# The rows of experts 0 to 29 added under the last expert, the last two experts' tokens scattered over the output

## The reference

```python
x = x + merged @ w_o
x = x + hier_moe(rmsnorm(x, norm_ffn), ...)

def expert_block(args):
    xb, e = args
    return (jax.nn.silu(xb @ w_gate[e]) * (xb @ w_up[e])) @ w_down[e]
...
y = jnp.zeros((t + 1, d), jnp.float32).at[row_tok].add(out.astype(jnp.float32) * row_w[:, None])
```

## Time and profile before

| what | value |
|---|---|
| median of 3 runs | 2049.8 us (2048.38 to 2050.29) |
| the profiled execution | 2054.24 us |
| its span | 2052.4 us |
| PE busy over the span | 1842.6 us, 90% |
| DVE busy over the span | 1283.2 us, 63% |
| ACT busy over the span | 1006.8 us, 49% |
| POOL busy over the span | 639.4 us, 31% |

### The profile page before, as it was taken

How to read it: one execution, slowest core, us unless ns; L and a number is a source line. 1 busy time by engine, 2 the same in 40 slices (tenths; PEclk the granted TensorE clock), 3 DMA queues, 4 the chain that set the end, 5 groups by cost and what they waited for, 6 DMA issues and landing times. The chain is left out here.

```text
span 2052.4 us, 26125 instructions
## 1 busy us (share of the span) xinstructions
PE 1842.6 (90%) x9426; PEld 1420.9 (69%) x9426; DVE 1283.2 (63%) x1351; ACT 1006.8 (49%) x1579; POOL 639.4 (31%) x368
## 2 busy tenths in 40 slices
PE   4898999999999779899999898985999999999991
PEld 3777787787787645677888786444677777777771
DVE  2677866875884835433344354124888888888883
ACT  4244543533444431355675420122577787777761
POOL 5247646746754933100134431000010111111000
PEclk7999999999999978899999999986999999999996
DMA  3243452424335442231155444512899999999985
GB/s 110 66 128 91 118 141 80 129 85 131 109 107 147 134 160 57 70 126 37 44 183 168 145 154 150 229 72 84 302 355 374 372 375 366 378 370 372 375 301 199
DMA packets 228110, 379.50 MB, mean 185 GB/s; under 512 B 14576, under 2 KB 176624, under 8 KB 203312
## 3 DMA queue, kind: packets, MB, share of 16 engines
q1 hardware_dynamic: 220272, 363.45, 51.8%
q0 software_dynamic: 7168, 12.60, 1.8%
q10 hardware_dynamic: 576, 2.18, 0.3%
HBM read 333.94 MB, written 55.25 MB: 190 GB/s over the span
## 5 line engine op out<-in xcount | busy, mean ns | idle before, releaser
L2011 DVE TENSOR_TENSOR e_w_low<-e_raw,e_w_high 128x2048 fp32r<-128x2048 f32 x190 | 426.5, 2286 | 63.3 <-ACT e_w_high L2007 63.3
L523 POOL TENSOR_TENSOR w_w_low<-w_raw,w_w_high 128x1024 fp32r<-128x1024 f32 x92 | 250.4, 2722 | 456.0 <-ACT w_w_high L518 456.0
L2007 ACT ACTIVATE e_w_high<-e_raw 128x2048 fp32r<-128x2048 f32 x190 | 349.9, 1914 | 0.0
L185 PE MATMUL bank<-h_high,w_w_high 128*128 128x512 f32 (+1 forms) x912 | 320.7, 352 | 31.9 <-ACT ssd_conv_in L802 16.7
L185 PE MATMUL bank<-h_low,w_w_high 128*128 128x512 f32 (+1 forms) x912 | 312.2, 342 | 0.0
L185 PE MATMUL bank<-h_high,w_w_low 128*128 128x512 f32 (+1 forms) x912 | 311.7, 342 | 0.0
L185 PEld LDWEIGHTS bank<-h_high,w_w_high 128*128 128x128 f32 x912 | 178.4, 196 | 65.0 <-issue 29.9
L2023 PE MATMUL bank<-e_w_high,e_xT_high 128*96 128x512 f32 x512 | 206.8, 404 | 3.2 <-DVE e_xT_low L2101 1.6
L2023 PE MATMUL bank<-e_w_high,e_xT_low 128*96 128x512 f32 x512 | 203.2, 397 | 0.0
L2023 PE MATMUL bank<-e_w_low,e_xT_high 128*96 128x512 f32 x512 | 202.3, 395 | 0.0
L946 DVE SCALAR_TENSOR_TENSOR ssd_xc<-ssd_conv_in,ssd_conv_p,ssd_xc 128x774 f32<-128x774 f32 x144 | 194.7, 1352 | 10.8
(11 more groups left out here) (282 smaller groups left out, 3582.4 us busy)
## 6 DMA issues: line engine op xcount, KB each, us to landing
e_raw<-in_w_gate SPq DMA_DIRECT2D x64, 1024.0 KB, 7.6
e_raw<-in_w_up SPq DMA_DIRECT2D x64, 1024.0 KB, 7.6
e_raw<-in_w_down SPq DMA_DIRECT2D x64, 1024.0 KB, 6.9
w_raw<-in_w_in SPq DMA_DIRECT2D x68, 512.0 KB, 4.1
ssd_decays<-decay_sums SPq DMA_DIRECT2D x48, 512.0 KB, 6.6
projected<-ssd_side SPq DMA_DIRECT2D x33, 384.0 KB, 2.5
w_raw<-in_w_out_ssm SPq DMA_DIRECT2D x16, 512.0 KB, 4.1
y_ssd<-ssd_y SPq DMA_DIRECT2D x24, 256.0 KB, 2.4
```

The costliest lines, as they stand in the source:

```text
L185: last = pe.matmul(out, lhs[k][a], rhs[k][b], start=(k == 0 and m == 0), stop=(k == n - 1 and m == 2))
L523: pool.tensor_tensor(self.pair[u].low[:, :, :], self.raw[u][:, :, :], self.pair[u].high[:, :, :].bitcast(F32), ALU.subtract).then_inc(self ...
L2007: act.activation(pair[n].high[:, :], core.raw[c][:, :], ACT.Copy).then_inc(high_ok, 1)
L2011: dve.tensor_tensor(pair[n].low[:, :], core.raw[c][:, :], pair[n].high[:, :].bitcast(F32), ALU.subtract).then_inc(low_ok, 1)
```

## The change

It has four parts.

1. SP waits for the scatters of experts 0 to 29 only, and loads each tile of `y_rows` into the raw buffer that comes free next while the last expert runs (`ROW_AT`, `ROW_FREE`). To make room, the last expert's two w_down chunks go to raw buffers 0 and 1 (`load_chunk(..., into=c)`), and their rounding and lowering moves ahead in ACT's and DVE's program of the last expert.
2. The twelve additions are split: tiles 0 to 2 go to POOL, 3 to 5 to DVE (`add_rows`).
3. Experts 30 and 31 no longer write `y_rows`. For their tokens the whole result is made apart, in the expert's slots: POOL gathers the token's x1 row (from the new table `x1_rows`, stored in `mix_and_route`) and the row of the token's other choice, and DVE adds these two and y. Since a token may have both experts, y of expert 30 also goes to a table of its own, `y_late` (zeroed as `y_rows` is), from which expert 31 gathers. The indices for all that are made by eight small DVE operations (`late_rows`).
4. When all six tiles are stored, POOL scatters these rows over the stored output, expert 30's first, two DMAs each (one for each sequence; indices outside a sequence are skipped), and waits for each pair.

The core of the diff:

```diff
                 def zeros(c):
-                    rows = core.y_rows[:, c * ZW:(c + 1) * ZW].rearrange("(b p) z -> p b z", p=P)
+                    for table in (core.y_rows, core.y_late):
+                        rows = table[:, c * ZW:(c + 1) * ZW].rearrange("(b p) z -> p b z", p=P)
...
                         sp.dma_start(core.h2_rows[at:at + P, :], h2[t % 2][:, :]).then_inc(h2_out[t % 2], 16)
+                    sp.dma_start(core.x1_rows[t * P:(t + 1) * P, :], x[:, t, :]).then_inc(x1_out, 16)
...
+            if last:
+                for c in range(2):
+                    round_chunk(act, END[c], down(e, c, True), c, NEXP)
             if not first:
                 act_out(act, e - 1, 1 - u, i - (1 - u))
...
+            else:
+                for c in range(2):
+                    lower_chunk(dve, END[c], down(e, c, True), c)
             dve.wait_ge(hh_ok, e + 1)
...
+        def late_rows(dve):
...
+            then(dve.tensor_copy(late[0][:, :], core.slot_row[:, NEXP - 2:NEXP]))
+            then(dve.tensor_scalar(late[1][:, :], late[0][:, :], float(TOK), float(TOK), ALU.is_ge, ALU.mult))
+            then(dve.tensor_tensor(late[0][:, :], late[0][:, :], late[1][:, :], ALU.subtract))
+            dve.tensor_copy(late_token[:, :], late[0][:, :])
+            then(dve.scalar_tensor_tensor(late[1][:, :], late[1][:, :], -1.0, late[0][:, :], ALU.mult, ALU.add))
+            dve.tensor_scalar(late_other[:, :], late[1][:, :], float(TOK), None, ALU.add)
+            then(dve.tensor_scalar(late[2][:, :], late[0][:, :], float(SEQS[0]), NO_ROW, ALU.is_lt, ALU.mult))
+            dve.scalar_tensor_tensor(late_second[:, :], late[0][:, :], -float(SEQS[0]), late[2][:, :],
+                                     ALU.add, ALU.add).then_inc(late_ok, 1)
...
+        def late_store(pool, v):
+            for s, index in enumerate((late_token, late_second)):
+                pool.indirect_dma_start(
+                    out=core.out[s][0], out_offset=bass.IndirectOffsetOnAxis(ap=index[:, v:v + 1], axis=0),
+                    in_=x[v][:, :], in_offset=None,
+                    bounds_check=SEQS[s] - 1, oob_is_err=False).then_inc(late_stored, 16)
...
+        def add_rows(eng, t, done):
+            eng.wait_ge(pair_in[t], 16)
+            for n in range(2):
+                last = eng.tensor_tensor(core.x1[:, t, :], core.x1[:, t, :],
+                                         core.raw[ROW_AT[t]][:, n * D:(n + 1) * D], ALU.add)
...
+        POOL_TILES = tuple(range(NT // 2))
+        ROW_AT = (2, 3, 4, 5, 0, 1)
+        ROW_FREE = (gate_up(NEXP - 1, 2), gate_up(NEXP - 1, 3), down(NEXP - 2, 0), down(NEXP - 2, 1),
+                    down(NEXP - 1, 0, True), down(NEXP - 1, 1, True))
...
-                sp_expert(sp, NEXP - 1, ahead=0)
-                sp.wait_ge(low_ok, 6 * NEXP)
+                for c in range(2):
+                    sp.wait_ge(low_ok, gate_up(NEXP - 1, c) + 1)
+                    load_chunk(sp, core, NEXP - 1, 4 + c, into=c)
                 for u in range(2):
-                    sp.wait_ge(y_out[u], 16 * (NEXP // 2))
+                    sp.wait_ge(y_out[u], 16 * (NEXP // 2 - 1))
                 rows = core.y_rows.rearrange("(n t p) d -> t p n d", n=2, p=P)
                 for t in range(NT):
-                    sp.dma_start(core.raw[t][:, :].rearrange("p (n d) -> p n d", n=2), rows[t]).then_inc(pair_in[t], 16)
-                for t in range(NT):
-                    sp.wait_ge(sum_ok, t + 1)
+                    sp.wait_ge(low_ok, ROW_FREE[t] + 1)
+                    sp.dma_start(core.raw[ROW_AT[t]][:, :].rearrange("p (n d) -> p n d", n=2), rows[t])\
+                        .then_inc(pair_in[t], 16)
+                for t in (0, 1, 3, 2, 4, 5):
...
                     sp.dma_start(core.out_tile(t), core.x1[:, t, :]).then_inc(stored, 16)
-                sp.wait_ge(stored, 16 * NT)
...
-                for e in range(NEXP):
+                for e in range(NEXP - 2):
                     pool_expert(pool, e)
+
+                pool.wait_ge(late_ok, 1)
+                for u in range(2):
+                    pool.wait_ge(y_out[u], 16 * (NEXP // 2 - 1))
+                for v in range(2):
+                    pool.wait_ge(x_tr, NEXP - 1 + v)
+                    late_gather(pool, x[v], core.x1_rows, late_token[:, v:v + 1], TOK, base_in[v])
+                    late_gather(pool, other[v], core.y_rows, late_other[:, v:v + 1], 2 * TOK, base_in[v])
+                add_rows(pool, 0, pool_sum_ok)
...
+                add_rows(pool, 1, pool_sum_ok)
+                pool.wait_ge(y_out[0], 16 * (NEXP // 2))
+                pool.wait_ge(based, 2)
+                late_gather(pool, other[1], core.y_late, late_other[:, 1:2], 2 * TOK, late_in)
+                add_rows(pool, 2, pool_sum_ok)
+                pool.wait_ge(stored, 16 * NT)
+                for v in range(2):
+                    pool.wait_ge(final_ok, v + 1)
+                    late_store(pool, v)
+                    pool.wait_ge(late_stored, 32 * (v + 1))
...
+                late_rows(dve)
...
+                for v in range(2):
+                    dve.wait_ge(base_in[v], 32)
+                    dve.tensor_tensor(x[v][:, :], x[v][:, :], other[v][:, :], ALU.add).then_inc(based, 1)
+                dve.wait_ge(y_ok, NEXP - 1)
+                dve.drain()
+                dve.tensor_tensor(x[0][:, :], x[0][:, :], y[0][:, :], ALU.add).then_inc(final_ok, 1)
+                for t in range(len(POOL_TILES), NT):
+                    add_rows(dve, t, dve_sum_ok)
+                dve.wait_ge(late_in, 16)
+                dve.tensor_tensor(x[1][:, :], x[1][:, :], other[1][:, :], ALU.add)
+                dve.wait_ge(y_ok, NEXP)
+                dve.drain()
+                dve.tensor_tensor(x[1][:, :], x[1][:, :], y[1][:, :], ALU.add).then_inc(final_ok, 1)
```

More of the change, by code:

```diff
@@ L1103, in zeros @@
                 def zeros(c):
[L1104 to L1106 removed]
+                    for table in (core.y_rows, core.y_late):
+                        rows = table[:, c * ZW:(c + 1) * ZW].rearrange("(b p) z -> p b z", p=P)
+                        sp.dma_start(rows, core.zeros[:, :].unsqueeze(1).to_broadcast([P, 2 * NT, ZW]))\
+                            .then_inc(core.zero_out, 16)
                 for i in range(ATT_SIDES):
@@ L1952, in weight_chunks, with load_chunk @@
     return [sb(f"e_raw{c}", [P, CHUNK_COLS]) for c in range(CHUNKS)]
-def load_chunk(sp, core, e, c):
+def load_chunk(sp, core, e, c, into=None):
+    into = c if into is None else into
     name, k = (("w_gate", KD), ("w_up", KD), ("w_down", KE))[c // 2]
     rows = core.expert_rows(name, e, k)[:, (c % 2) * (k // 2):(c % 2 + 1) * (k // 2), :]
-    sp.dma_start(core.raw[c][:, :].rearrange("p (k n) -> p k n", k=k // 2), rows).then_inc(core.raw_in[c], 16)
+    sp.dma_start(core.raw[into][:, :].rearrange("p (k n) -> p k n", k=k // 2), rows).then_inc(core.raw_in[into], 16)
 def experts(core):
@@ L2170, in overflows, with then @@
             dve.tensor_copy(core.overflow[:, :], owner[0:1, :])
+        def late_rows(dve):
+            def then(last):
+                dve.drain()
[8 more added lines that the diff above has]
+                                     ALU.add, ALU.add).then_inc(late_ok, 1)
@@ new lines, in late_gather @@
+        def late_gather(pool, into, table, index, rows, done):
+            pool.indirect_dma_start(
+                out=into[:, :], out_offset=None, in_=table[:, :],
+                in_offset=bass.IndirectOffsetOnAxis(ap=index, axis=0),
+                bounds_check=rows - 1, oob_is_err=False).then_inc(done, 16)
+        def late_store(pool, v):
+            for s, index in enumerate((late_token, late_second)):
+                pool.indirect_dma_start(
+                    out=core.out[s][0], out_offset=bass.IndirectOffsetOnAxis(ap=index[:, v:v + 1], axis=0),
+                    in_=x[v][:, :], in_offset=None,
+                    bounds_check=SEQS[s] - 1, oob_is_err=False).then_inc(late_stored, 16)
@@ L2172, in experts @@
+        def add_rows(eng, t, done):
[3 more added lines that the diff above has]
+                                         core.raw[ROW_AT[t]][:, n * D:(n + 1) * D], ALU.add)
+                if n == 0:
+                    eng.drain()
+            last.then_inc(done, 1)
         LAST = NEXP // 2 - 1
         END = [slot(0, c) for c in range(2)]
+        POOL_TILES = tuple(range(NT // 2))
+        ROW_AT = (2, 3, 4, 5, 0, 1)
@@ L2221, in _ @@
                 act_expert(act, NEXP - 1, 1, LAST, last=True)
-                for c in range(2):
-                    round_chunk(act, END[c], down(NEXP - 1, c, True), 4 + c, NEXP - 1)
                 act_out(act, NEXP - 1, 1, LAST, last=True)
@@ L2246, in _ @@
                 dve_expert(dve, NEXP - 1, 1, last=True)
-                for c in range(2):
-                    lower_chunk(dve, END[c], down(NEXP - 1, c, True), 4 + c)
-                for t in range(NT):
-                    dve.wait_ge(pair_in[t], 16)
```

(13 more changed lines are left out.)

28 lines of the change are left out of this document (23 added, 5 removed).

## The result

The changed kernel takes 2056.2 us, the median of eight runs, against 2050.5 us for the kernel before, also of eight: a ratio of 1.0029 with a 95% interval of 1.0017 to 1.0041. It is 5.7 us slower. The prediction was 2045.1 us, 2037 to 2052.

The account below looks back on a forecast made before the run. PE bounds the experts to about 2001, then a tail of single steps: additions to 2026.3, store 2029.5, scatters 2040.7, with 5.5 us of end 2046.2, with late_rows 2047.7; against the median 2045.1 us, range 2037 to 2052.

Parts of the forecast that it names:

- From 1997.8 on one of the two engines holds the path nearly always: Tail additions: POOL and DVE run two-input SBUF work one after the other, so all of it adds up, to 2026.3.
- sum of 28.5 us: Tail: DVE's two subtractions 4.5, POOL's six additions 14.2, DVE's six additions and three row sums 9.8 us.
- Four gathers on POOL at 1.25 us each: POOL ahead of its additions: four gather issues at 1.25 us each, so its first addition comes at 1998 to 1999.
- rival 2: POOL's six DMA issues wait for DVE's operation, up to 2.28 us each; 1.3 us less, no change; chance 0.07.
- DVE's order: DVE in the tail: free at 1997.8, its six additions and three row sums take turns with POOL until 2026.
- I count none of these 3.6 us: Last expert: early w_down starts PE's down product at 2003.4, not 2007.02, but this was given no gain.
- near 2005: Last expert: the time at which PE should start its last product.
- The chain at the end: Behind the last addition: last store 3.1 us, then two scatter pairs of 5.6 us each, 11.2, ending at 2040.7.
- Rival 3: End DMAs land as in full queues, 8.6 a store, 7.4 a scatter: 8.8 us slower, 2058.6; chance 0.10.
- late_rows: Second expert: eight small DVE operations cost 1.5 us, bounds 0 and 2.2; PE's 4.94 us pause should be 6.4.

Follow-up runs that it names:

- e1_sem: The changed kernel with a semaphore in place of POOL's drain between its two additions of a tile; 2053.6 us, ratio to before 1.0016.
- e7_dve_first: e3_dve with a POOL drain in every expert's turn and DVE's row sums moved in among its additions; 2045.2 us.
- e3_dve: The changed kernel with all twelve additions on DVE, POOL keeping only gathers and scatters; 2057.8 us.
- e2_drain: The changed kernel with one more POOL drain, behind the four gathers and ahead of the first addition; 2066.0 us.
- e4_late_gathers: The changed kernel with POOL's four gathers issued only after DVE's last two subtractions; 2070.6 us.
- e6_loop: The changed kernel with a POOL drain in every expert's turn, in POOL's idle time; 2058.3 us, ratio to before 1.0028.

## Why the prediction was wrong

- **The step that failed: "From 1997.8 on one of the two engines holds the path nearly always".** The sum of 28.5 us took additions and nothing between them. It gave no price to the drain in `add_rows`, which between POOL's additions waits for POOL's own DMAs: 9.19, 0.38 and 1.82 us. Against the forecast the last addition came 10.1 us late (52.2, not 42.1); with the drain replaced (e1_sem) the last store is issued 7.9 us earlier. The exclusion that it did count was right: the engines do take turns.
- **"Four gathers on POOL at 1.25 us each"** was mis-sized: with their gaps they took 10.3 us (1990.90 to 2001.15), not 5. This is rival 2, given 0.07 on the evidence of 32 issues at 0.911 to 0.945 us "beside DVE subtractions". None of the 32 is beside a subtraction with two SBUF inputs: while the scatter of 1986.08 is issued DVE lowers from PSUM (e_hT_low, 0.56 us from 1985.68), and its next subtraction with two SBUF inputs starts at 1987.48, and so it is in every turn. Those rows priced an issue that meets nothing. Nor is the hold bounded by one operation, 2.28 us, as the rival had it: the third gather met two. What the 5 us cost by themselves was not measured: the drain and DVE waited for the last gather's landing anyway.
- **DVE's order.** The forecast had DVE add from 1998 on whenever POOL did not; but its additions stand behind a row sum that waited 5.37 us for a gather. Moving them (e7_dve_first) took some 5.1 us off e3_dve's tail beyond the 4.8 that the drains in the turns gave at its end.
- **"I count none of these 3.6 us"**, for the early w_down, was right for the changed kernel, where expert 31's rows are ready at 2007.20 and used at 2031.16. But the rows come 6.2 us earlier, not 3.6: PE's last product starts 19.2 us behind the copy, where "near 2005" is 20.8, and runs at clock 1.00. On the path of the kernel before they were worth all of it.
- **The chain at the end** was right in kind. The last store took 4.38 us and, since three were released together, landed 5.3 us behind the last addition, where the sum has 3.2 and its bounds allow 5.0; the scatter pairs are 5.26 us apart, forecast 5.6. Rival 3, with 8.6 us for the store and 7.4 for each scatter, did not occur.
- **late_rows**: PE's pause is 6.35 us (forecast 6.4), 4.94 before. From PE's first turn to the copy of expert 29's rows it takes 569.12 us and not 568.33, so 0.8 of the 1.5 is left.

Open: in the changed kernel 2.7 us of the 9.19 lie behind the landing of the last gather, as in e2_drain and e4_late_gathers, in e6_loop 0.3. DVE's two row sums run beside them, but they need not be the cause: in the kernel before, with DVE idle, the drain of 2017.4 also ends 2.6 us behind the last landing (2021.18). DMAs worked off late fit, but at 0.083 us each the 62 to 64 DMAs would take twice as long, and in which order a drain waits and works off no run here separates. Open too is why PE's clock began low in two of thirteen runs, and why e2_drain, e3_dve and e4_late_gathers are longer than their tails say.

## What to carry to other kernels

A fence that is cheap on one engine can be dear on another: on an engine that issues DMAs, order two of its operations by a semaphore, and put a drain where it idles, so that little is left for the end. Take the price of an operation from rows in which its neighbours do what they will do after the change, and issue POOL's indirect DMAs where DVE runs nothing with two SBUF inputs. And time each part of a large change alone: here the smallest part held all of the gain, and the rest, as first written, took back more than that.

## What the hardware showed that I had not expected

- POOL's drain waits until POOL's own gathers and scatters have landed, and takes 0.083 us for each DMA issued since the last drain, even when all have landed: 4.96 us for 60, 1.52 for 18. Without drains in between, the drain at the end of the stage pays it: 5.78 us for 70 DMAs, 0.38 for 4.
- An indirect DMA's issue on POOL that begins beside an fp32 operation with two SBUF inputs on DVE takes up to 4.75 us, and ends 0.80 to 0.86 us behind such an operation; without one it takes 0.91 to 0.98.
- Behind the same wait of 1.70 us PE's last 24 matmuls took 5.8 us in eleven runs (granted clock 1.00), and 7.4 us in two, the first eight of them at the lower level.
